# Four attentions of 64-column heads: values stationary on column halves, probabilities divided before they are turned, outputs split straight from their bank

## What is computed

```python
# even mixer of layer 0 (called eA in the kernel)
s = q @ k.T * scale + cum_logf[q] - cum_logf[k]          # causal
p = softmax(s);  o = p @ v                               # 8 heads of 64
# odd mixer of layer 1 (oA)
s = q @ k.T * scale + bias_by_distance;  p = softmax(s);  o = p @ v
# third layer: window of 128 with a sink logit (sA), and block attention (mA);
# both have 8 query heads and 2 key/value heads
p = softmax(concat([s, sink]))[..., :-1];  o = p @ v
```

## Time and profile before

| | |
|---|---|
| time, median of 3 runs | 1627.97 us (1625.81 to 1628.63) |
| span of the profiled execution | 1626.7 us |
| TensorE busy | 1600.1 us, 98% of the span |
| VectorE busy | 1106.4 us, 68% |
| ScalarE busy | 862.0 us, 53% |
| granted TensorE clock, mean | 0.997 of full speed |
| weights read | 288.29 MB from HBM, 180 GB/s |

### The profile page before, as it was taken

How to read it: one execution, slowest core, us unless ns; L and a number is a source line. 1 busy time by engine, 2 the same in 40 slices (tenths; PEclk the granted TensorE clock), 3 DMA queues, 4 the chain that set the end, 5 groups by cost and what they waited for, 6 DMA issues and landing times.

```text
span 1626.7 us, 21211 instructions
## 1 busy us (share of the span) xinstructions
PE 1600.1 (98%) x8058; PEld 1337.7 (82%) x8058; DVE 1106.4 (68%) x1761; ACT 862.0 (53%) x1324; POOL 227.5 (14%) x351
## 2 busy tenths in 40 slices
PE   8999999999999999999999999999999999999998
PEld 6888877788888888888889888888889877888886
DVE  6775788867655556555596776655568997776566
ACT  5554556855545445444555555544454457454444
POOL 2499901000000000000000000000014442100000
PEclk9999999999999999999999999999999999999999
DMA  9766656445466565656655453565675554556653
GB/s 277 237 209 218 209 157 192 157 142 156 133 191 187 188 184 178 193 182 193 208 174 156 151 181 116 182 186 189 191 262 164 166 157 137 187 193 190 188 188 109
DMA packets 187543, 295.22 MB, mean 181 GB/s; under 512 B 13510, under 2 KB 108144, under 8 KB 186160
## 3 DMA queue, kind: packets, MB, share of 16 engines
q1 hardware_dynamic: 183264, 275.93, 54.6%
q0 software_dynamic: 3888, 17.60, 3.4%
q10 hardware_dynamic: 288, 0.33, 0.1%
HBM read 288.29 MB, written 5.25 MB: 180 GB/s over the span
## 4 chain that ended last, share of the span: by engine, by line
PE 86%; DVE 7%; ACT 3%; issue 2%; POOL 1%; DMA 0%; SPq 0%; DVEq 0%; ACTq 0%
PE b L445 25%; PE b L447 24%; PE b L446 24%; PE b L646 4%; DVE wlo L1655 2%; PE b L648 2%; ACT whi L1100 1%; PE b L669 1%; PE b L511 1%; PE b L899 1%; PE b L881 1%; PE b L608 1%; PE b L561 1%; PE b L527 1%; ACT R L1189 1%
## 5 line engine op out<-in xcount | busy, mean ns | idle before, releaser
L1655 DVE TENSOR_TENSOR wlo<-raw,whi 128x1024 fp32r<-128x1024 f32 (+1 forms) x523 | 648.5, 1243 | 436.5 <-ACT whi L1100 435.2
L1100 ACT ACTIVATE whi<-raw 128x1024 fp32r<-128x1024 f32 (+1 forms) x523 | 550.0, 1053 | 557.8 <-PE b L447 522.3
L445 PE MATMUL b<-whi,hT 128*128 128x512 f32 (+1 forms) x1040 | 413.4, 397 | 10.5 <-DVE wlo L1655 8.9
L447 PE MATMUL b<-whi,hT 128*128 128x512 f32 (+1 forms) x1040 | 405.1, 390 | 0.0
L446 PE MATMUL b<-wlo,hT 128*128 128x512 f32 (+1 forms) x1040 | 404.6, 389 | 0.0
L445 PE MATMUL b<-whi,oT 128*128 128x512 f32 x672 | 265.0, 394 | 0.0
L447 PE MATMUL b<-whi,oT 128*128 128x512 f32 x672 | 262.0, 390 | 0.0
L446 PE MATMUL b<-wlo,oT 128*128 128x512 f32 x672 | 261.6, 389 | 0.0
L445 PEld LDWEIGHTS b<-whi,hT 128*128 128x128 f32 x1040 | 196.1, 189 | 55.2 <-DVE wlo L1655 10.3
L447 PEld LDWEIGHTS b<-whi,hT 128*128 128x128 f32 x1040 | 196.0, 188 | 41.6
L446 PEld LDWEIGHTS b<-wlo,hT 128*128 128x128 f32 x1040 | 196.5, 189 | 37.9
(11 more groups left out here) (343 smaller groups left out, 1864.0 us busy)
## 6 DMA issues: line engine op xcount, KB each, us to landing
raw<-in_ffn_w_in SPq DMA_DIRECT2D x350, 256.0 KB, 3.2
raw<-in_ffn_w_out SPq DMA_DIRECT2D x88, 512.0 KB, 3.3
raw<-in_w_ff SPq DMA_DIRECT2D x64, 512.0 KB, 4.1
raw<-in_w_in SPq DMA_DIRECT2D x36, 512.0 KB, 3.7
raw<-in_x_w_kv SPq DMA_DIRECT2D x32, 512.0 KB, 4.1
raw<-in_even_w_in SPq DMA_DIRECT2D x24, 512.0 KB, 3.9
raw<-in_odd_w_in SPq DMA_DIRECT2D x24, 512.0 KB, 3.8
raw<-in_x_w_q SPq DMA_DIRECT2D x16, 512.0 KB, 4.0
```

The lines of the kernel that those rows point to most:

```text
L445: T.matmul(out, ah, bh, start=start, stop=False, skip_group_check=skip)
L447: return T.matmul(out, al, bh, start=False, stop=stop, skip_group_check=skip)
L1100: E.activation(K.whi[j % NSPLIT][:, 0:n], K.raw[j % NRAW][:, 0:n], ACT.Copy).then_inc(*S.whi.done(j))
L1655: V.tensor_tensor(K.wlo[j % NSPLIT][:, 0:n], K.raw[j % NRAW][:, 0:n], K.whi[j % NSPLIT][:, 0:n].bitcast(F32), ALU.subtract).then_inc(*S.wl ...
```

## The change

1. `weigh_two` takes the place of `weigh`, three times per attention: it does two items at once. The values (128x64) are stationary, for the even head on array columns 0 to 63, for the odd one on columns 64 to 127, and the turned probabilities move (128 columns). 8 products (L605) take the place of 2 x 4. The output comes out already turned: bank 7 holds features by rows.
2. So `out_turn` is left out for the four attentions. `row_highs` (ACT) and `row_lows` (DVE) split bank 7 directly, one 128x4x128 operation each per 128 rows.
3. Division can no longer be done per row on the output. The probabilities are divided before they are turned: in eA and oA by DVE (`divided`: reciprocal and one 128x512 product for each item), in sA and mA by ACT (`item_divided`: 4 copies of 128x128 or 2 of 128x256 with the reciprocal as scale), after DVE's `inverse_sums`. `weighed` is left out.
4. The turn of an item stands later by about one piece, and so do `probs` and the products.

```diff
-    def weigh(a, i, ready):
+    def weigh_two(a, i, ready):
...
-                ins = T.matmul(banks[7][:, 64 * h:64 * h + 64], K.pT[K.buf(a.name, i)][:, (k * nkt + kt) * P:(k * nkt + kt + 1) * P],
-                               a.values(h, kt), start=(kt == 0), stop=(kt == nkt - 1))
+                for u in range(2):
+                    ins = T.matmul(banks[7][64 * u:64 * u + 64, 64 * h:64 * h + P], a.values(h + u, kt),
+                                   K.pT[K.buf(a.name, i + u)][:, (k * nkt + kt) * P:(k * nkt + kt + 1) * P],
+                                   start=(kt == 0), stop=(kt == nkt - 1), skip_group_check=True)
...
-            if s - 3 in SCORED_AT:
-                i = SCORED_AT[s - 3]
-                weigh(A["mA" if i >= 6 else "sA"], i % 6, ready(i)[1])
-            if s - 1 in SCORED_AT:
-                i = SCORED_AT[s - 1]
+            if SCORED_AT.get(s - 4, 0) % 2:
+                i = SCORED_AT[s - 4]
+                weigh_two(A["mA" if i >= 6 else "sA"], i % 6 - 1, ready(i)[1])
+            if s - 2 in SCORED_AT:
+                i = SCORED_AT[s - 2]
                 prob_turn("mA" if i >= 6 else "sA", i % 6, 4)
...
+    def item_divided(name, i):
+        t, heads = ITEMS[i]
+        nh, nk = len(heads), P * (t + 1)
+        s3, rc = K.Sb[K.buf(name, i)][:, 0:nh * nk].rearrange("p (h k) -> p h k", h=nh), K.stat(("rc", name, i), nh)
+        act.wait_ge(*S.recip.at((name, i)))
+        for k in range(nh):
+            ins = E.activation(s3[:, k, :], s3[:, k, :], ACT.Copy, scale=rc[:, k:k + 1])
+        ins.then_inc(*S.divided_a.done((name, i)))
...
-            if s - 2 in SCORED_AT:
-                i = SCORED_AT[s - 2]
+            if s - 3 in SCORED_AT:
+                i = SCORED_AT[s - 3]
                 probs("mA" if i >= 6 else "sA", i % 6)
+            if s - 1 in SCORED_AT:
+                i = SCORED_AT[s - 1]
+                item_divided("mA" if i >= 6 else "sA", i % 6)
...
+    def inverse_sums(name, i):
+
+        t, heads = ITEMS[i]
+        rc, sums = K.stat(("rc", name, i), len(heads)), K.stat(("sum", name, t), 8)[:, heads[0]:heads[-1] + 1:2]
+        dve.wait_ge(*S.exped.at((name, i)))
+        if A[name].sink:
+            dve.wait_ge(*S.exped.at((name, i, "sink")))
+            V.tensor_tensor(sums, sums, K.stat(("es", name, i), len(heads)), ALU.add).then_inc(*S.dve_own.done())
+            before()
+        V.reciprocal(rc, sums).then_inc(*S.recip.done((name, i)))
+
+    def divided(name, i):
...
+        inverse_sums(name, i)
+        dve.wait_ge(*S.recip.latest())
+        V.tensor_tensor(s3, s3, rc.unsqueeze(2).to_broadcast([P, nh, nk]), ALU.mult).then_inc(*S.divided.done((name, i)))
...
+            if s - 1 in SCORED_AT:
+                i = SCORED_AT[s - 1]
+                inverse_sums("mA" if i >= 6 else "sA", i % 6)
             if s - 1 in DRIVEN_AT:
                 turn_forth(DRIVEN_AT[s - 1])
...
-        gemm("kv02", *copied("kv02"), None, {0: lambda: (weigh_a(0), turn_a(1)),
-                                             1: lambda: (weigh_a(1), out_b(0), turn_a(2), score_a(4)),
-                                             2: lambda: (out_b(1), turn_a(3), score_a(5)), 3: lambda: (weigh_a(2), turn_a(4))})
+        gemm("kv02", *copied("kv02"), None, {0: lambda: turn_a(1),
+                                             1: lambda: (out_b(0), weigh_a(0), score_a(4)),
+                                             2: lambda: (out_b(1), turn_a(2), score_a(5)), 3: lambda: turn_a(3)})
```

More of the change, by code:

```diff
@@ L106 @@
     "recip", "weighed", "final", "dve_own", "trig", "scan", "conv", "gated", "bt", "proj", "back", "forth",
-    "pool_own", "gained", "blended", "zeroed", "table", "decayed", "turned_back", "turned_forth", "mixed_p", "divided",
+    "pool_own", "gained", "blended", "zeroed", "table", "decayed", "turned_back", "turned_forth", "mixed_p", "divided", "divided_a",
 )
@@ L132, in __init__ @@
          S.scan, S.conv, S.gated, S.bt, S.proj, S.back, S.forth, S.pool_own, S.gained, S.blended, S.zeroed, S.table,
-         S.decayed, S.turned_back, S.turned_forth, S.mixed_p, S.divided) = (s[n] for n in SIGNALS)
+         S.decayed, S.turned_back, S.turned_forth, S.mixed_p, S.divided, S.divided_a) = (s[n] for n in SIGNALS)
         S.x_in = ((s["x00"], s["x01"]), (s["x10"], s["x11"]))
@@ L607, in weigh @@
             for kt in range(nkt):
[L608 to L612 removed]
+                for u in range(2):
+                    ins = T.matmul(banks[7][64 * u:64 * u + 64, 64 * h:64 * h + P], a.values(h + u, kt),
+                                   K.pT[K.buf(a.name, i + u)][:, (k * nkt + kt) * P:(k * nkt + kt + 1) * P],
+                                   start=(kt == 0), stop=(kt == nkt - 1), skip_group_check=True)
+        ins.then_inc(*S.mixed.done((a.name, i), (a.name, i + 1)))
+        if i in (0, 4):
+            free[7] = (S.alo.at(("rows", a.name, t)),)
     def ffn(f, extra={}, following=None, second_piece={}):
@@ L841, in weigh_a @@
         def weigh_a(i):
-            weigh(a, i, v_ready)
+            weigh_two(a, i, v_ready)
         def turn_a(i):
@@ L1485, in odd @@
             if p == 0:
-                probs("oA", 3)
                 for m in range(2):
@@ new lines, in divided, with row_lows @@
+    def divided(name, i):
+        t, heads = ITEMS[i]
+        nh, nk = len(heads), P * (t + 1)
+        s3, rc = K.Sb[K.buf(name, i)][:, 0:nh * nk].rearrange("p (h k) -> p h k", h=nh), K.stat(("rc", name, i), nh)
+        inverse_sums(name, i)
+        dve.wait_ge(*S.recip.latest())
+        V.tensor_tensor(s3, s3, rc.unsqueeze(2).to_broadcast([P, nh, nk]), ALU.mult).then_inc(*S.divided.done((name, i)))
+    def row_lows(name, t):
+        k0 = A[name].first_out
+        hi, lo = (a[:, k0:k0 + 4, P * t:P * t + P] for a in K.oT)
+        dve.wait_ge(*S.ahi.at(("rows", name, t)))
+        V.tensor_tensor(lo, banks[7][:, :].rearrange("p (k q) -> p k q", k=4), hi.bitcast(F32),
+                        ALU.subtract).then_inc(*S.alo.done(("rows", name, t), *([("o", name, 0), ("o", name, 1)] if t else [])))
@@ L2241, in even @@
             elif p == 2:
+                divided("eA", 0)
                 item(1)
@@ L2244, in even @@
                 diff_weighed()
+            elif p == 3:
+                divided("eA", 1)
         for p in pieces("kv02"):
@@ L2252, in even @@
                 out_lows("eB", 4, (0,), 124)
+                divided("eA", 2)
             elif p == 2:
                 item(4)
-                weighed("eA", 0)
+                divided("eA", 3)
                 head_scale("kv01", 2, 256, False, None, "ak")
+                row_lows("eA", 0)
             elif p == 3:
@@ L2259, in even @@
                 item(5)
+                divided("eA", 4)
         project_x("e", "eo", "x0", 16, (2, 3, 0, 1), {
-            2: lambda: weighed("eA", 1), 3: lambda: out_lows("eA", 0)})
+            0: lambda: divided("eA", 5), 3: lambda: row_lows("eA", 1)})
     def cross(l):
@@ L2376, in odd @@
                 item(0)
+            elif p == 2:
+                divided("oA", 0)
         for p in pieces("ch"):
@@ L2379, in odd @@
                 item(1)
+            elif p == 1:
+                divided("oA", 1)
             elif p == 3:
                 item(2)
-                weighed("oA", 0)
         for p in pieces("cb"):
             if p == 0:
+                divided("oA", 2)
                 gate_u()
+                row_lows("oA", 0)
                 tap(0)
@@ L2391, in odd @@
                 tap(2)
+            elif p == 3:
+                divided("oA", 3)
         for p in pieces("kv11"):
@@ L2401, in odd @@
                     low_halves(K.oT, 2 * m, rows(4 + 2 * m), ("o", "oc", m))
+            elif p == 2:
+                divided("oA", 4)
         for p in pieces("kv12"):
@@ L2406, in odd @@
             elif p == 1:
+                divided("oA", 5)
                 head_rstd("kv11", 2, 256, "m")
@@ L2409, in odd @@
                 head_scale("kv11", 2, 256)
-            elif p == 3:
-                weighed("oA", 1)
         head_copy("kv11", K.xkT, 4, [K.gain(118), K.gain(119)])
-        project_x("o", "oo", "x1", 56, (0, 1, 2, 3), {0: lambda: out_lows("oA", 4)})
+        project_x("o", "oo", "x1", 56, (0, 1, 2, 3), {0: lambda: row_lows("oA", 1)})
     def second():
@@ L2509, in second @@
                 state_out(DRIVEN_AT[s - 5] // 4)
-            if s - 1 in OUT_AT:
-                a, k0, g = OUT_AT[s - 1]
-                out_lows(a, k0, (g,))
+            if SCORED_AT.get(s - 5, 0) % 6 in (1, 5):
+                i = SCORED_AT[s - 5]
+                row_lows("mA" if i >= 6 else "sA", int(i % 6 == 5))
             if s == 2:
```

106 lines of the change are left out of this document (36 added, 70 removed).

## The result

The changed kernel takes 1630.1 us (median of 11 runs, 1629.06 to 1631.83) against 1626.66 for the kernel before, timed beside it (11 runs, 1625.67 to 1628.63): a ratio of 1.0018, 95% interval 1.0011 to 1.0026. That is slower by 3.4 us, about 0.2%. The forecast was 1629.4 and "same"; the interval doesn't hold 1, so the loss is small but can be told from no change.

The account below looks back on a forecast made before the run. PE was taken to pace layer 1, DVE much of layers 0 and 3. Terms -2.6 + 1.5 + 2.5 = +1.4 us on a 1626.7 span gave 1628.1, plus 1.3 to the median: 1629.4 us; 8-in-10 range 1620 to 1636.

Parts of the forecast that it names:

- five signs: Trace signs in PE's new groups and layers 0, 1 and 3 that would show the forecast's own case, 1626 to 1632, chance 0.35.
- the group's price: On PE, all four attentions: the new groups of 8 products would show at 1.1 to 1.2 us.
- DVE's standing: Layer 3: DVE would be idle for 0.5 us before the small additions of items 0, 1, 6 and 7.
- the turn's wait in layer 0: Layer 0: PE would wait for DVE's division before a turn; kv02's second piece +2.0 us.
- the wait of over 3 us for the gate: Layer 3: PE would wait for the gate by 3 us or more.
- Layer 1, -2.6: oA: PE sets the pace, so its 2.6 us saving comes in full; DVE's added 3.4 us stay hidden.
- Layer 0, +1.5: eA: DVE has no room, so its divisions delay PE, net +1.5 us; bounds -2.6 to +3.2.
- the delay falls to some 1.5: Layer 0: PE's savings cut the 3.2 us delay at kv02's third piece to 1.5 by the output projection.
- Layer 3, +2.5: sA, mA: DVE's chain, then ACT's, make PE 3.2 us late at the gate, less 0.7; bounds -5 to +6.
- Rival B: All layers: PE's saving arrives; 1621 us if two thirds of the 10.5 come, 1617 if all; chance 0.25.
- Rival D: Layer 3: DVE's new wait for exponentials, 0.5 us late for 8 items, costs +4: 1633.5 us; chance 0.3.
- Rival C: New groups: column halves don't overlap, a pair costs 2.2 us, PE loses 0.4 a pair; 1635 us; chance 0.1.

Follow-up runs that it names:

- e2: The kernel before with the change in oA (layer 1) alone; 1624.83 us, ratio 0.9984.
- e10: The changed kernel with eA (layer 0) as before and layer 3 in the three altered orders of e7; 1621.41 us, ratio 0.9961.
- e9: The changed kernel with layer 0's dividing products moved from DVE to ACT, DVE making only the inverse sums; 1632.74 us, ratio 1.0035.
- e13: e7 with item 1 of eA divided on DVE behind `wlo` of kv02's first piece and its turn a piece later; 1625.05 us, ratio 0.9987.
- e12: The changed kernel with unused transposes of the identity on PE ahead of the pieces at s = 12 and s = 32; 1628.07 us, ratio 1.0003.
- e1: The changed kernel with ACT's division of layer 3's items 1 and 11 behind the copy of mA's queries and gate 2; 1629.24 us, ratio 1.0010.
- e8: The changed kernel with layer 3's division left out altogether, PE's turns waiting for the exponentials; 1625.24 us, ratio 0.9987.
- e7: The changed kernel, layer 3 reordered: ACT's divisions of items 1 and 11 and `probs` of item 10 later, DVE's inverse sums behind the forward rotation; 1624.19 us, ratio 0.9983.
- e4: The changed kernel with each group's products head by head, so the column halves run one after the other; 1633.34 us, ratio 1.0036.

## Why the prediction was right, step by step

The time was right within 0.7 us, and the way the loss arises in each layer too, but part of the closeness is luck. The change was forecast as +1.4 us and measured as +3.4. The forecast added its +1.4 to 1627.97, the median of three runs; over 11 runs the kernel before takes 1626.66, 1.3 less. The 1.3 us that the forecast put between span and median lie between the span and the time of the same execution (1628.9 and 1630.23 in the changed kernel); by the same 1.3 the profiled execution of the kernel before took 1628.0, an estimate, and was one of its longer ones. The terms fell 2.0 short: 0.8 in layer 0 and 1.4 in layer 3, less 0.2 in layer 1. All five signs that the forecast named for its case came: the group's price, layer 1, DVE's standing, the turn's wait in layer 0 and the wait of over 3 us for the gate.

- **Layer 1, -2.6.** Right: -2.8, no wait of PE, DVE's additions hidden (e2 shows it alone). The group costs 1.22 with its gap, as forecast. The 0.2 that are left over are traced to no row.
- **Layer 0, +1.5.** The path was as told: the turn waits for DVE (it began at 318.90; less this trace's -1.1 that is the 320 of the forecast), and the third piece is 3.2 late, as forecast. The step that failed is "the delay falls to some 1.5": it is 2.9 at the output projection (1.82 in place of -1.12 in the same comparison) and 2.3 behind it. That the change in eA is what costs it is shown by e10; that it is the length of the chain through both engines, and not DVE's amount of work, fits e9 and e13 but isn't shown step by step.
- **Layer 3, +2.5.** The maximum of item 11 starts at 1349.87, 1.6 us late for a start of the stage that was 1.7 early (forecast 1.9); PE behind the gate is 4.86 late (forecast 3.2), and 0.97 are given back (forecast 0.7). In e12, where the clock doesn't fall, PE is 3.45 late there. So the term that was missing is PE's clock, 1.4 us; without it layer 3 costs 2.5, as forecast.
- **Missed: the copy of mA's queries.** ACT's divisions were said to lie in its waits for DVE. Item 1's doesn't: PE waited 2.55 us for the copy behind it, and 1.4 with the division moved (e1) or left out (e8). Removing the stall alone brought little, since by s = 21 DVE has taken up the difference.
- **Rival B** is half true. PE's saving can arrive in layer 3, as the forecast's text denied ("it can't run ahead of `wlo`"): 4.3 us in e8 up to s = 32, and 1.6 over the layer with the division in a better order in e7. **Rival D**'s wait is there, 0.52 to 0.55 us for each of the four items of four heads and not for eight, and e7's order removes it from DVE. **Rival C** is excluded by the group's price and by e4. (Its sum has -2.6 + 3.0 as +0.3; it is 0.4. Rival D's 1629.4 + 4 is 1633.4. Neither changes a verdict.)

## What to carry to other kernels

When work moves to another engine, list for each place what stands behind it in that engine's program and who waits for it: 0.6 us of ACT ahead of a gate was worth 2.1 here, and 0.1 behind it. Make a change that has several places one place at a time: three of the four attentions together, in a better order, gave 5 us, where all four in the first order lost 3. A wait of PE can cost more than its length, since its clock may fall in it, so look at the granted clock behind each long wait before adding up the work. Such a fall comes in some executions and not in others: compare the mean granted clocks of the timed runs before you lay a difference of 1 or 2 us to the code. And take the time that a forecast change is added to from many runs: the median of three was 1.3 us off here.
